# One encoder layer on one core: the last product as seven block products in two groups of steps

## What is computed

```python
h = rmsnorm(x, norm_ffn)                       # (512, 1024)
gu = h @ ffn_w_gate_up                         # (1024, 2 * 2816)
x = x + (silu(gu[:, :2816]) * gu[:, 2816:]) @ ffn_w_down   # (2816, 1024)
out = rmsnorm(x, final_norm)
```

## Time and profile before

| what | value |
|---|---|
| median of three runs | 1078.31 us (1076.4 to 1078.4) |
| span of the profiled execution | 1077.6 us |
| TensorE busy | 1042.8 us, 97% of the span |
| share of TensorE in the chain that ended last | 93% |
| mean granted TensorE clock | 0.991 of full speed |

### The profile page before, as it was taken

How to read it: one execution, slowest core, us unless ns; L and a number is a source line. 1 busy time by engine, 2 the same in 40 slices (tenths; PEclk the granted TensorE clock), 3 DMA queues, 4 the chain that set the end, 5 groups by cost and what they waited for, 6 DMA issues and landing times.

```text
span 1077.6 us, 14413 instructions
## 1 busy us (share of the span) xinstructions
PE 1042.8 (97%) x5926; PEld 867.7 (81%) x5926; DVE 522.1 (48%) x731; ACT 380.0 (35%) x570; POOL 135.0 (13%) x207
## 2 busy tenths in 40 slices
PE   8999999999989998999999999999999999999995
PEld 7889798856678897888888888778888888888884
DVE  6775446567666788464251525453333333322313
ACT  6535545654432212442232312343222222311312
POOL 4000000525763231000000000000000000000201
PEclk9999999999999999999999999999999999999998
DMA  8322320000100013114232336323333333233201
GB/s 294 127 80 87 117 69 2 1 1 11 21 12 1 2 40 118 59 40 137 78 106 70 118 98 215 98 63 94 95 101 89 107 82 113 79 117 109 90 17 78
DMA packets 104001, 87.18 MB, mean 81 GB/s; under 512 B 13110, under 2 KB 93698, under 8 KB 103937
## 3 DMA queue, kind: packets, MB, share of 16 engines
q1 hardware_dynamic: 102288, 81.80, 25.1%
q0 software_dynamic: 1488, 4.40, 1.1%
q10 hardware_dynamic: 160, 0.07, 0.0%
HBM read 83.64 MB, written 2.62 MB: 80 GB/s over the span
## 4 chain that ended last, share of the span: by engine, by line
PE 93%; DVE 4%; ACT 1%; issue 1%; DMA 0%; POOL 0%; DVEq 0%; ACTq 0%; POOLq 0%
PE psum L901 24%; PE psum L902 24%; PE psum L903 24%; PE psum L1206 2%; PE psum L1213 2%; PE psum L1226 1%; PE psum L1305 1%; PE psum L1361 1%; PE psum L1180 1%; PE psum L1349 1%; PE psum L1278 1%; PE psum L1335 1%; PE psum L1166 1%; PE psum L1100 1%; PE psum L1029 1%
## 5 line engine op out<-in xcount | busy, mean ns | idle before, releaser
L1975 DVE TENSOR_TENSOR w_lo<-w_raw,w_hi 128x2048 fp32r<-128x2048 f32 (+2 forms) x81 | 167.5, 2068 | 232.5 <-ACT w_hi L1518 232.5
L901 PE MATMUL psum<-hT_hi,w_hi 128*128 128x512 f32 (+1 forms) x712 | 278.1, 391 | 2.1 <-DVE hT_lo L2019 1.0
L903 PE MATMUL psum<-hT_hi,w_lo 128*128 128x512 f32 (+1 forms) x712 | 277.2, 389 | 0.0
L902 PE MATMUL psum<-hT_lo,w_hi 128*128 128x512 f32 (+1 forms) x712 | 277.0, 389 | 0.0
L1518 ACT ACTIVATE w_hi<-w_raw 128x2048 fp32r<-128x2048 f32 (+2 forms) x82 | 141.4, 1725 | 157.2 <-PE psum L903 145.0
L901 PEld LDWEIGHTS psum<-hT_hi,w_hi 128*128 128x128 f32 (+1 forms) x712 | 133.2, 187 | 31.3 <-issue 2.3
L903 PEld LDWEIGHTS psum<-hT_hi,w_lo 128*128 128x128 f32 (+1 forms) x712 | 133.2, 187 | 28.2
L902 PEld LDWEIGHTS psum<-hT_lo,w_hi 128*128 128x128 f32 (+1 forms) x712 | 133.3, 187 | 27.8
L1975 DVE TENSOR_TENSOR psum<-gate_act,psum 128x512 f32<-128x512 f32 x22 | 15.3, 696 | 119.4 <-PE psum L903 119.4
L901 PE MATMUL psum<-w_hi,act_hi 128*128 128x512 f32 x176 | 68.5, 389 | 0.0
L902 PE MATMUL psum<-w_lo,act_hi 128*128 128x512 f32 x176 | 68.5, 389 | 0.0
(11 more groups left out here) (311 smaller groups left out, 1577.5 us busy)
## 6 DMA issues: line engine op xcount, KB each, us to landing
w_raw<-in_w_in_dram SPq DMA_DIRECT2D x23, 1024.0 KB
w_raw<-in_ffn_w_gate_up_dram SPq DMA_DIRECT2D x44, 512.0 KB
w_raw<-in_ffn_w_down_dram SPq DMA_DIRECT2D x10, 1024.0 KB
w_raw<-in_mem_w_kv_dram SPq DMA_DIRECT2D x4, 1024.0 KB
w_raw<-in_w_out_dram SPq DMA_DIRECT2D x4, 1024.0 KB
x_tok<-in_x_dram SPq DMA_DIRECT2D x4, 512.0 KB, 5.6
w_raw<-in_w_branch_mla_dram SPq DMA_DIRECT2D x4, 512.0 KB
w_raw<-in_w_branch_dn_dram SPq DMA_DIRECT2D x4, 512.0 KB
```

Source lines behind the costliest of these rows:

```text
L901: pe.matmul(o, s_hi, m_hi, start=first, stop=False)
L902: pe.matmul(o, s_hi, m_lo, start=False, stop=False)
L903: return pe.matmul(o, s_lo, m_hi, start=False, stop=last)
L1975: return dve.tensor_tensor(o, a, b, op)
```

## The change

The last product is computed by Strassen's seven block products. The activations are seen as a 2x2 of blocks (token half by half of the 2816), the weight as a 2x2 (half of the 2816 by column half). Instead of eight block products there are seven, of sums and differences of blocks:

- Two groups of steps. A step takes one pair of f tiles (i and i + 11); there are 11 pairs, so 22 steps (`STEPS`). In the first group each step feeds products 1, 4, 7 and 5, in the second 2, 3 and 6. A product takes 2 token tiles x 3 passes, so a step is 24 matmuls of 128x512 in the first group and 18 in the second: 11 x 24 + 11 x 18 = 462.
- The sums. GpSimd makes five sums of 128x256 for each pair of activation tiles (`pair_sums`), and for each step three sums of 128x512 of weight tiles in the first group, two in the second (`weight_sums`). Both inputs of each of them lie in SBUF.
- The splits. (Of the two `step_split` below the first is ScalarE's, the second VectorE's; `sp` is SyncE, `pool` GpSimd.) ScalarE and VectorE split the sums in `step_split`: 128x2048 of weights and 128x1024 of activations for a step of the first group, 128x1536 and 128x768 for one of the second. `act_hi` and `act_lo` are gone; VectorE writes the plain activations to `acts`.
- The loads. Each step loads three weight tiles of 256 KB into one of three buffers `dw`; the first two lie in the old `w_raw` ring, the third where `hT_hi` was. In all 22 x 3 x 256 KB in place of 44 x 256 KB.
- The adds. VectorE adds or subtracts each finished product to one or two blocks of `x1` (`take`): ten adds of two tiles before step 12, two more pairs later, and ten tile adds after the last step. Products of the second group reuse banks of the first.
- GpSimd's load of `fin_w` moves behind `weight_sums(9)`; the order of the last norm is that of `FINAL`.

```diff
+NP = NF // 2
+GU_ORDER = [i + NP * u for i in range(NP) for u in range(2)]
+STEPS = 2 * NP
+FIRST_FOUR, LAST_THREE = (1, 4, 7, 5), (2, 3, 6)
...
+        acts = v("acts", [P, NP, 7, 256], 0)
+        dw = [at(f"dw{i}", [P, 6, 512], F32, o) for i, o in enumerate((ring, ring + 12 * KB, hbase))]
...
+        def step_free(eng, s):
+            if s < 2:
+                filled(eng, ("u", GU_ORDER[NF - 2 + s]))
+            elif s - 2 == NP - 1:
+                filled(eng, ("M", FIRST_FOUR[-1], 1))
+            else:
+                eng.wait_ge(step_used, s - 1 - (s - 2 > NP - 1))
...
+            for s in range(STEPS):
+                if s < 2:
+                    sp.wait_ge(w_lo_done, NB - 1 + s)
+                elif s == 2:
+                    filled(sp, ("u", GU_ORDER[NF - 1]))
+                else:
+                    sp.wait_ge(dw_lo, s - 2)
+                i = s % NP
+                places = ((4, i, 0), (5, NP + i, 0), (3, NP + i, 1)) if s < NP else ((0, i, 0), (4, i, 1), (5, NP + i, 1))
+                for unit, f, half in places:
+                    sp.dma_start(dw[s % 3][:, unit, :],
+                                 ffn_w_down[0][f * P:(f + 1) * P, 512 * half:512 * half + 512]).then_inc(dw_landed[s % 3], 16)
...
+            def weight_sums(s):
+                w = lambda n: dw[s % 3][:, n, :]
+                pool.wait_ge(dw_landed[s % 3], 48 * (s // 3 + 1))
+                if s < NP:
+                    pool.tensor_tensor(w(0), w(4), w(3), ALU.add).then_inc(dw_sums, 1)
+                    pool.tensor_tensor(w(1), w(5), w(4), ALU.subtract).then_inc(dw_sums, 1)
+                    pool.tensor_tensor(w(2), w(5), w(3), ALU.add).then_inc(dw_sums, 1)
+                else:
+                    pool.tensor_tensor(w(1), w(4), w(5), ALU.subtract).then_inc(dw_sums, 1)
+                    pool.tensor_tensor(w(2), w(0), w(4), ALU.add).then_inc(dw_sums, 1)
+
+            for i in range(NP - 1):
+                pair_sums(i)
+            for s in range(2):
+                weight_sums(s)
+            pair_sums(NP - 1)
+            for s in range(2, STEPS):
+                weight_sums(s)
...
+            def step_split(s):
+                wh, _, ah, _ = step_in(s)
+                n = factors(s)
+                step_free(act, s)
+                act.wait_ge(dw_sums, step_sums(s))
+                A(wh[:, 0:512 * n], dw[s % 3][:, 0:n, :].rearrange("p a b -> p (a b)")).then_inc(dw_hi, 1)
+                act.wait_ge(act_sums, 5 * (s % NP + 1))
+                first = 3 if s < NP else 0
+                A(ah[:, 0:n, :], acts[:, s % NP, first:first + n, :]).then_inc(a_hi_done, 1)
...
+            def step_split(s):
+                wh, wl, ah, al = step_in(s)
+                n = factors(s)
+                dve.wait_ge(dw_hi, s + 1)
+                tt(wl[:, 0:512 * n], dw[s % 3][:, 0:n, :].rearrange("p a b -> p (a b)"), f32(wh[:, 0:512 * n]),
+                   ALU.subtract).then_inc(dw_lo, 1)
+                dve.wait_ge(a_hi_done, s + 1)
+                first = 3 if s < NP else 0
+                tt(al[:, 0:n, :], acts[:, s % NP, first:first + n, :], f32(ah[:, 0:n, :]), ALU.subtract).then_inc(a_lo_done, 1)
...
+            for s in range(1, STEPS):
+                if s == NP + 1:
+                    take(1, 0, 0, ALU.add, x1_added)
+                    take(1, 1, 1, ALU.add, None)
+                    taken(1)
+                    take(4, 0, 0, ALU.add, x1_added)
+                    take(4, 1, 0, ALU.add, None)
+                    taken(4)
+                    take(7, 0, 0, ALU.add, None)
+                step_split(s)
...
+            take(6, 1, 1, ALU.add, x2_ready)
             final_means(0)
-            add_glu(1, 3)
```

More of the change, by code:

```diff
@@ L39 @@
 NF = D_FF // P
+NP = NF // 2
+GU_ORDER = [i + NP * u for i in range(NP) for u in range(2)]
+STEPS = 2 * NP
+FINAL = [(half, 2 * row + t) for half, row in ((0, 0), (0, 1), (1, 0), (1, 1)) for t in range(2)]
+FIRST_FOUR, LAST_THREE = (1, 4, 7, 5), (2, 3, 6)
 LEVELS = 7
@@ L112, in weight_blocks @@
             out.append((("wo", half, kk), [rows(w_out, 512 * half, 512, 4 * kk, 4)], 4, 512))
-    for f in range(NF):
+    for f in GU_ORDER:
         out.append((("gu", f), [rows(w_gu, f * P, P), rows(w_gu, D_FF + f * P, P)], KD, 256))
[L115 to L118, removed]
     return out
@@ L273, in psum_uses @@
         turn(("h2T", k), every)
-    for f in range(NF):
+    for f in GU_ORDER:
         turn(("g", f), every)
         turn(("u", f), every)
-    for half in range(2):
-        for t in range(NT):
-            use(("down", half, t), 4 * half + t)
+    for group in (FIRST_FOUR, LAST_THREE):
+        for i, m in enumerate(group):
+            for t in range(2):
+                use(("M", m, t), 2 * i + t)
     return uses
@@ L887, in _ @@
                 c = slice(512 * half, 512 * half + 512)
[L888 to L890 removed]
+                pool.wait_ge(x2_ready, n + 1)
+                pool.tensor_tensor(y_out[t][:, c], x1[:, t, c], fin_w[:, c], ALU.mult).then_inc(xw_ready, 1)
         @block.tensor
@@ L1487, in _, with down_product, step_ready @@
                 by_feature(("u", f), ("gu", f), P, hT_hi, hT_lo)
[L1488 to L1505, removed]
+            def down_product(s, m, a_unit, w_unit):
+                wh, wl, ah, al = step_in(s)
+                c = slice(512 * w_unit, 512 * w_unit + 512)
+                first, last = s % NP == 0, s % NP == NP - 1
+                for t in range(2):
+                    key = ("M", m, t)
+                    if first:
+                        claim(pe, key)
+                    r = slice(t * P, (t + 1) * P)
+                    ins = product(bank(key), ah[:, a_unit, r], al[:, a_unit, r], wh[:, c], wl[:, c], first, last)
+                    if last:
+                        ins.then_inc(full(key), 1)
+                return ins
+            def step_ready(s):
+                pe.wait_ge(dw_lo, s + 1)
+                pe.wait_ge(a_lo_done, s + 1)
+            for s in range(STEPS):
+                step_ready(s)
+                for m, a_unit, w_unit in ((1, 1, 0), (4, 0, 1), (7, 3, 2), (5, 2, 3)) if s < NP else ((2, 1, 0), (3, 0, 1), (6, 2, 2)):
+                    ins = down_product(s, m, a_unit, w_unit)
+                if s % NP != NP - 1:
+                    ins.then_inc(step_used, 1)
         @block.scalar
@@ L1944, in final_scale @@
             def final_scale(t):
[L1945 to L1952, removed]
+                A(y_out[t], y_out[t], scale=rstd[:, t:t + 1]).then_inc(y_ready[t], 1)
+            for s in range(1, STEPS):
+                step_split(s)
+                if s == 18:
+                    for n in range(2):
+                        final_squares(n)
             root_tables()
-            for t in range(NT):
-                final_squares(1, t)
-                if t == 2:
+            for n in range(2, 8):
+                final_squares(n)
+                if n == 6:
                     root("final", small[:, 2, 0:2], small[:, 1, 0:2], 0)
@@ L2567, in _ @@
                 released(dve, ("g", f))
[L2568 to L2584, removed]
+                in_two = lambda ap: ap.rearrange("p (a b) -> p a b", a=2)
+                dst = acts[:, f % NP, 0:4, :].rearrange("p (a u) b -> p u a b", u=2)[:, f // NP]
+                tt(dst, in_two(gate_act[:, n % 2, :]), in_two(bank(key)), ALU.mult).then_inc(free(key), 1)
@@ L2585, in final_means, with take @@
+            def take(m, row, half, op, step):
+                for t in range(2):
+                    key = ("M", m, t)
+                    filled(dve, key)
+                    c = x1[:, 2 * row + t, 512 * half:512 * half + 512]
+                    ins = tt(c, c, bank(key), op)
+                    ins.then_inc(free(key) if step is None else step, 1)
             def final_means(b):
-                dve.wait_ge(ssq_ready, 3 * NT + NM + 2 * b + 2)
+                dve.wait_ge(ssq_ready, 2 * NT + NM + 2 * b + 6)
@@ L2587, in final_means, with taken @@
                 dve.scalar_tensor_tensor(out=small[:, 1, 2 * b:2 * b + 2], in0=small[:, 0, 2 * b:2 * b + 2], scalar=EPS,
                                          in1=small[:, 0, NT + 2 * b:NT + 2 * b + 2], op0=ALU.add, op1=ALU.add).then_inc(ms_ready, 1)
-            add_glu(1, 1)
-            add_glu(1, 2)
+            def taken(m):
+                for t in range(2):
+                    released(dve, ("M", m, t))
+            for s in range(1, STEPS):
+                if s == NP + 1:
[6 more added lines that the diff above has]
+                    take(7, 0, 0, ALU.add, None)
+                step_split(s)
+                if s == NP + 2:
+                    taken(7)
+                    take(5, 0, 0, ALU.subtract, x2_ready)
+                if s == NP + 3:
+                    take(5, 0, 1, ALU.add, None)
@@ L2592, in _ @@
+            taken(5)
+            take(2, 1, 0, ALU.add, x2_ready)
+            take(2, 1, 1, ALU.subtract, None)
+            taken(2)
```

(5 more changed lines are left out.)

78 lines of the change are left out of this document (52 added, 26 removed).

## The result

The changed kernel takes 1095.72 us (median of 4 runs, 1094.99 to 1095.78) against 1077.96 us before (4 runs): ratio 1.0162, 95% interval 1.0147 to 1.0176. The forecast was 1097, slower. It is slower by 1.6%, clear of the interval. The span of the profiled execution is 1094.0 us, its time 1095.74. In every execution listed with both, the time is 1.7 to 1.9 us above the span. The profiled execution of the kernel before, with its span of 1077.6, so took about 1079.3, which is 1.3 above the median.

The account below looks back on a forecast made before the run. TensorE was taken to bound the kernel, busy for 97% of the span. 66 matmuls fewer save 15.0 us, waits lose 30, the tail adds 3.6: 18.6 more, about 1097 us, range 1084 to 1110.

Parts of the forecast that it names:

- step 1 starts: After gate-up: step 1's split waits for the last up product and pair sums; activations ready at 6.5 us.
- step 2 starts: Early down: five pair sums and three weight sums queued on GpSimd delay the split; start 18.8 us, TensorE idle 6.8.
- a step of 3 to 10: First group: GpSimd's three sums plus VectorE's subtractions, 7.30 us less four prepared starts, 6.82 against TensorE's 5.44.
- step 12 starts: Start of second group's later steps: split stands behind all ten adds and needs 1.76 + 0.96 us more.
- a step of 13 to 21: Second group: two GpSimd sums plus VectorE's 2.72 us, 5.24 less prepared starts, 4.76 against TensorE's 4.08.
- The exclusion: Down: VectorE instructions with two SBUF inputs and GpSimd's SBUF-reading sums do not overlap, so their times add; costing little: 0.12.
- Steps 10 and 11: Group change: banks come free through ten adds of 0.69 us, so step 11 takes 6.9 us instead of 4.08.
- The second group: Steps 13 to 21: both engines' summed times set the step, 4.76 us; latency alone 4.4 against 4.08.
- The clock: Before step 2: 6.8 idle us may lower TensorE's clock once, costing under 2 us, mostly hidden; chance 0.05.
- The tail: After the last matmul: ten tile adds end 2.8 us later, waiting products about 0.8 more; 3.6 us in all.
- The sum: Whole kernel: +15.0 us in down and 3.6 after it, 18.6 more, about 1097 us.
- The range: Whole time: 1084 to 1110 for 8 in 10; the forecast's own 1088 to 1104, from sum prices, with 0.64.

Follow-up runs that it names:

- e1: Changed kernel with GpSimd's weight sums from step 2 on replaced by memsets of the same tiles, which read nothing: 1084.51 us, ratio 1.0061 to the kernel before.
- e2: Changed kernel with the weight sums of steps 2 to 21 moved from GpSimd to VectorE, ahead of the previous step's split: 1082.09 us, ratio 1.0036.
- e5: Changed kernel with weight sums on VectorE (steps 13 and 14 on GpSimd) and next step's activations split behind this step's weights: 1075.42 us, ratio 0.9977.
- e7: Changed kernel with only the activations of step s + 1 split behind the weights of step s, sums still on GpSimd: 1090.66 us, ratio 1.0119.
- e8: e5 with GpSimd's first two products with fin_w held until VectorE has issued the last split: 1073.95 us, ratio 0.9971.
- e6: e5 with GpSimd's last five pair sums spread behind splits of steps 2 to 6, and weight sums of steps 12 and 15 also on GpSimd: 1078.06 us.

## Why the prediction was right

Times from the first matmul of down.

| term | forecast | measured |
|---|---|---|
| matmul pitch and count | 0.2267 x 462 | 462, same pitch between dips of the clock |
| step 1 starts | 6.5 | 6.4 |
| step 2 starts | 18.8 | 18.4 |
| a step of 3 to 10 | 6.82 | (73.90 - 18.41) / 8 = 6.94 |
| step 12 starts | 87.8 | 85.6 |
| a step of 13 to 21 | 4.76 | (133.24 - 89.74) / 9 = 4.83 |
| down | 134.7 | 133.2 |
| tail, more than before | 3.6 | 3.05 |

- *The exclusion* was the term that decided in the first group, and e1 and e2 show it from two sides: without GpSimd reading, or with all reading on one engine, the steps fall to the latency of 5.64, and with that shortened too (e5) to TensorE's 5.44. Shortening the latency alone moves the first group hardly (e7). The earlier trace rows had it in three meetings. The mean of 6.94 hides steps of 5.52 to 8.01: in the changed kernel the splits of steps 4 to 7 and 10 start when TensorE frees the buffers and those of 3, 8 and 9 when the sums are ready, while GpSimd never idles; in e7 all wait for the sums.
- *Steps 10 and 11* were forecast 2.7 us too long (14.4 from the start of step 10 to that of step 12; measured 11.66). Ten adds in a row took 6.41 us and not 6.9 (0.64 each, their starts overlapping), and VectorE was through with step 11's split at 1022.9, 4.7 us before TensorE began step 11, so the adds began earlier than I had them.
- *The second group* is right in size by luck. The sum of both engines' times cannot set a step in which GpSimd idles over 1 us. What sets it is the latency with one link lengthened: from the end of step 14 (99.83) to the start of step 16 (105.41) lie 5.58 us; with step 16's own 4.21 that is 9.79 for two steps, the 4.89 by which steps 14 to 18 are apart. The forecast had 4.4 for this latency, without the 1.1 us by which a sum stretches `a_lo` (2.05 for 0.95). The two ways come out alike: where the latency is shortened, steps 18 to 21 of e7 are 4.73 apart, near the summed 4.76.
- *The clock*: I had one dip, mostly hidden. There were three: after 6.4 us of idle (the window from 965 shows 0.50), and in steps 8 and 10, after idle times of 2.5 and 2.2 us, with a granted clock of 0.53 and 0.54 in the windows behind (1006.8 to 1010.2 and 1020.4 to 1023.7). In each some nine matmuls run at a pitch of 0.43 us, 1.8 us of TensorE's time, part of which it would have waited anyway. No experiment separates this part. It is small: e7 has no dip in steps 3 to 10 and less latency, and its steps are only 0.15 us shorter. In e5 and e8 there is no dip in down, though step 2 still waits 2.4 us.
- *The tail*: the last add ended 3.3 us after the last matmul's slot, before 0.9, so 2.4 more (2.8 forecast), and the second means came 2.5 after it instead of 1.87.
- *The sum.* Against the span the forecast of 18.6 us more met 16.4, against the medians 17.8. The errors have both signs: the measured times are 0.9 us longer in steps 2 to 9 and 0.6 in steps 13 to 21, 2.7 shorter in steps 10 and 11 and 0.55 in the tail. That they cancel in part, and the forecast misses 1095.72 by only 1.3 us, is luck.
- *The range* of 1084 to 1110 was wide against a miss of 1.3 us. The narrower one, 1088 to 1104, does not follow from its own prices: 4 off and 19 more give 1093 to 1116, outside even the wide one. The price of a sum, 1.26 by the row of the same form, was measured as 1.28 to 1.30.

## What to carry to other kernels

Before giving an idle engine part of a busy one's work, look in the trace for an instruction of the one that stretches while the other runs; if there is one, add their times and compare with the step, whatever the busy shares say. The sum binds while neither queue idles; where one of them does, follow the chain from buffer to buffer instead, with each link at its stretched length. Read rates from start times: the pitch of 0.227 us, not the duration of 0.39, showed that 5.4 us were left where 10.9 had been. And work can be cheaper on the busier engine: e2 moved sums of 31 us onto VectorE and the kernel became 13.6 us faster.

## What the hardware showed that I had not expected

- GpSimd that only writes is not held back and holds nobody back (e1: memsets of 0.53 us beside subtractions of 2.29 and 1.22).
- Taking turns is not certain. In the changed kernel each waiter got in at the next end. In e6 one pair sum of 128x256, 0.74 us undisturbed, stood for 13.65 us while VectorE ran fourteen two-input instructions without a pause:

```profile
959.79 13.65 POOL L932 TENSOR_TENSOR acts<-acts 128x256 f32<-128x256 f32 x1 [20.80 <-DVE w_lo L2079]
973.41 2.78 POOL L934 TENSOR_TENSOR acts<-acts 128x256 f32<-128x256 f32 x1
```

```profile
962.48 2.29 DVE L2079 TENSOR_TENSOR w_lo<-dw,w_hi 128x2048 fp32r<-128x2048 f32 x1
964.68 1.22 DVE L2079 TENSOR_TENSOR a_lo<-acts,a_hi 128x1024 fp32r<-128x1024 f32 x1
965.82 1.89 DVE L2079 TENSOR_TENSOR dw<-dw 128x512 f32<-128x512 f32 x3
967.62 2.29 DVE L2079 TENSOR_TENSOR w_lo<-dw,w_hi 128x2048 fp32r<-128x2048 f32 x1
```

  All of these have their undisturbed lengths. Once GpSimd was in, at 973, its next sums and VectorE's splits stretched each other again, which is the loss at steps 5 to 7. What decides between turns and no turns stays open; no run separates it.
- TensorE's granted clock fell after idle times of 2.2 and 2.5 us between steps in the changed kernel, while 1.7 us before step 4 left it at full. But the length of the idle time does not decide: in e7 three idle times of 2.5 us (before steps 6, 8 and 10) were followed by full clock. And the kernel before had a fall at 225.6, with no pause longer than 0.83 us near it, where e8, with the same instructions there and nearly the same busy share before, had none. In this order: e7, two windows; the kernel before, two; e8, one (columns as in the earlier trace rows, the clock before the last two).

```profile
986.80:989.26 2.46, 0.15 (x2) 0.01 (x1) 2.46 (x2) 0.69 (x1) 2.46 (x2) 1.00 0.00 0
989.26:992.70 3.44, 3.44 (x15) 2.83 (x16) 2.48 (x2) 2.27 (x2) 3.44 (x3) 1.00 0.64 219
...
222.00:225.60 3.60, 2.66 (x11) 1.24 (x11) 3.60 (x6) 1.43 (x5) 0.00 (x0) 1.00 0.00 0
225.60:229.00 3.40, 3.40 (x16) 1.90 (x17) 2.43 (x4) 1.30 (x3) 1.22 (x2) 0.50 0.00 0
...
225.60:229.00 3.40, 3.40 (x28) 1.99 (x27) 2.28 (x5) 2.21 (x5) 1.23 (x2) 1.00 0.00 0
```

  So the same code has a fall in one execution and none in another; what decides stays open.
